# The last feed-forward stage: the high part of the weights passes once over 512 columns, and the bank's halves are added when it is read

## The chip, the cores and the metric

The kernel runs on one core of one Trainium2 chip. The metric is the device time of one execution in microseconds (us), the median of three runs. TensorE is called PE in the profile, VectorE DVE, ScalarE ACT, GpSimd POOL and SyncE SP.

## The reference

The reference is two model blocks in float32, one after the other, over 256 latent tokens of width 1024; the first also carries 256 context tokens. Each layer of the first block is a feed-forward, an attention and a feed-forward, each with a norm and with shifts, scales and gates made from a condition. Of its eleven parts only the feed-forward matters here:

```python
def rms(x):
    return x * lax.rsqrt(jnp.mean(x * x, axis=-1, keepdims=True) + EPS)

def modulate(h, shift, scale):
    return h * (1 + scale) + shift

def swiglu(h, wi, wo):                    # wi 1024 x 5632, wo 2816 x 1024
    g, u = jnp.split(h @ wi, 2, axis=-1)
    return (jax.nn.silu(g) * u) @ wo
```

The result is scaled by half of a gate and added to `x`. In the last layer of the first block the context isn't wanted any more after the attention, so the last feed-forward (`"post"`, layer 1) works on the 256 latent tokens alone. The second block (a recurrence, two sparse attentions and a table lookup of experts, twice) follows.

## The kernel before, in words

Tokens lie along the free dimension: `xT[:, m, :]` holds 128 features of 512 tokens, the latent ones first (`LAT` = 256), then the context (`TOK` = 512). The program is a chain of 27 stages. Each engine runs its own hand-written list, and all of them meet at the end of a stage (`end_phase`). The change touches one stage, number 9, `ffn("post", 1)`, the only feed-forward with `T == LAT`.

**Split products.** A float32 product is made of three matmuls in the type `fp32r`: operands are cut into a high part (`hi`, the rounded value) and a low part (`lo`, what is left), and w·h is w_hi·h_hi + w_hi·h_lo + w_lo·h_hi. `three` (L597) lists the pairs and `SplitWeights.mm` (L583, the matmul itself is L586) issues them into one PSUM bank. A block is one 128x128 piece of weights. A group is 8 blocks. ACT makes `w_hi` of a group (`SplitHi.ahead`, L539), DVE makes `w_lo` (`SplitLo.ahead`, L557), both four groups ahead of PE, in a ring of four (`split_ring`). A ring slot comes free when PE is two blocks into the next group. Weights come from HBM over SP's queue into `wt`, three tiles of two groups deep.

**The stage.** It has two halves of 33 groups. In a half, 11 pairs of groups come first: for each j, the gate (8 blocks over k, into a bank of `A_`) and the up projection (8 blocks, into a bank of `D_`). ACT applies silu to the gate's bank (L744), DVE multiplies it with the up bank (L761, `hid_raw`), ACT makes `hid_hi` (L750), DVE makes `hid_lo` (L768). Then 11 groups of the down projection: 8 outputs m, each 11 blocks over f, into banks of `D_`; the first m waits for each `hid_ready`. DVE adds each output to `xT` (`dve_residual`, L496). `h_hi` and `h_lo` have room for 512 columns; with `T == LAT` half of each is unused.

**Order on DVE and ACT.** Both lists go over the groups g in order. In an even g ACT takes silu of this gate and then splits group g+4; DVE only splits. In an odd g DVE multiplies, splits, and makes `hid_lo`; ACT splits and makes `hid_hi`. `step` (the `Stepper`) makes DVE or ACT wait for its own instruction to be done before it goes on, and other engines are told by `sem_inc` instructions behind it:

```python
step(dve.tensor_tensor(hid_raw[:, 0:T], s[:, 0:T], bank[:, 0:T], ALU.mult))
dve.sem_inc(silu_ring.free, 1)
dve.sem_inc(D_.free, 1)
dve.sem_inc(raw_ready.sem, 1)
```

Of the kernel before, what the change touches and what calls it, by code (L numbers as in the profile page):

```python
# [8 lines left out]
F32 = mybir.dt.float32  # L9
# [3 lines left out]
ALU = mybir.AluOpType  # L13
# [263 lines left out]
def model_kernel(nc, wstream, adastream, cond, vecs, consts, onehots, tokens, peer_uv, out):  # L277
    ctx = ExitStack()
    with ctx:
# [231 lines left out]
        w_hi_ready = signal("w_hi_ready")  # L511
        h_hi_ready = signal("h_hi_ready")
        raw_ready = signal("raw_ready")

        def groups_of(name, layer, cols, col=0):

# [45 lines left out]
        class SplitWeights:  # L562
# [20 lines left out]
            def mm(self, o, pairs, start, stop, inc):  # L583
# [5 lines left out]
                elif self.owed and not start:  # L589
                    ins.then_inc(split_ring.free, 1)  # L590
                    self.owed -= 1

            def close(self):
# [92 lines left out]
        def dve_split_norm(dve, step, groups, T):  # L686
            weights = SplitLo(dve, step, groups)
            dve.wait_ge(rstd_ready.sem, rstd_ready.due(dve))
            for k in range(DC + 2):
                if k < DC:  # L690
                    dve.tensor_tensor(hT[:, k, 0:T], xT[:, k, 0:T], rstd[:, 0:T], ALU.mult).then_inc(xn_ready.sem, 1)
                if k >= 2:
                    dve.wait_ge(h_hi_ready.sem, h_hi_ready.due(dve))
                    dve.tensor_tensor(h_lo[:, k - 2, 0:T], hT[:, k - 2, 0:T], h_hi[:, k - 2, 0:T].bitcast(F32),
                                      ALU.subtract).then_inc(h_ready.sem, 1)
# [11 lines left out]
        def pe_ffn(pe, W, mm, which, l, T):  # L707
            SW = SplitWeights(pe, W)
            pe_norm(pe, mm, T)
            for part in range(0, FC, HALF):  # L710
                for j in range(part, part + HALF):
                    for half, r in ((0, A_), (1, D_)):
                        pe.wait_ge(r.free, r.given_back())
                        bank = r.claim()
                        for k in range(DC):
                            if j == 0 and half == 0:
                                pe.wait_ge(h_ready.sem, h_ready.due(pe))
                            w = SW.next(f"ffn_{which}_wi", l, k * P, half * FF + j * P)
                            SW.mm(bank[:, 0:T], three(w, h_parts(k, 0, T)), k == 0, k == DC - 1,
                                  r.full if k == DC - 1 else None)  # L720
                for m in range(DC):
                    pe.wait_ge(D_.free, D_.given_back())
                    bank = D_.claim()
                    for f in range(HALF):
# [3 lines left out]
                        SW.mm(bank[:, 0:T], three(w, (hid_hi[:, f, 0:T], hid_lo[:, f, 0:T])), f == 0, f == HALF - 1,  # L728
                              D_.full if f == HALF - 1 else None)
            SW.close()  # L730

        def act_ffn(act, step, which, l, sub, T, first=False):
            if first:
                act.wait_ge(cond_loaded, 16)
                act.activation(silu_cc[:, :, :], silu_cc[:, :, :], ACT.Silu).then_inc(silu_done, 1)
                act.wait_ge(loaded.sem, loaded.due(act, FIRST_LOADS))
            weights = act_split_norm(act, step, ffn_groups(which, l), l, sub, T, first)
            for g in range(2 * HALF_GROUPS):
                i = g % HALF_GROUPS
                if i < GATED_GROUPS and i % 2 == 0:  # L740
                    act.wait_ge(A_.full, A_.filled())
                    act.wait_ge(silu_ring.free, silu_ring.given_back())
                    bank, s = A_.take(), silu_ring.claim()
                    step(act.activation(s[:, 0:T], bank[:, 0:T], ACT.Silu))  # L744
                    act.sem_inc(A_.free, 1)
                    act.sem_inc(silu_ring.full, 1)
                weights.ahead()
                if i < GATED_GROUPS and i % 2:
                    act.wait_ge(raw_ready.sem, raw_ready.due(act))
                    act.activation(hid_hi[:, i // 2, 0:T], hid_raw[:, 0:T], ACT.Copy).then_inc(hid_hi_ready.sem, 1)  # L750

        def dve_ffn(dve, step, which, l, sub, T, ada=(), first=False):
            ada = spread(ada, 2 * HALF_GROUPS)
            weights = (dve_first_norm if first else dve_split_norm)(dve, step, ffn_groups(which, l), T)
            for g in range(2 * HALF_GROUPS):
                i = g % HALF_GROUPS
                if i < GATED_GROUPS and i % 2:
                    dve.wait_ge(silu_ring.full, silu_ring.filled())
                    dve.wait_ge(D_.full, D_.filled())
                    s, bank = silu_ring.take(), D_.take()  # L760
                    step(dve.tensor_tensor(hid_raw[:, 0:T], s[:, 0:T], bank[:, 0:T], ALU.mult))  # L761
                    dve.sem_inc(silu_ring.free, 1)
                    dve.sem_inc(D_.free, 1)
                    dve.sem_inc(raw_ready.sem, 1)
                weights.ahead()
                if i < GATED_GROUPS and i % 2:
                    dve.wait_ge(hid_hi_ready.sem, hid_hi_ready.due(dve))
                    step(dve.tensor_tensor(hid_lo[:, i // 2, 0:T], hid_raw[:, 0:T],  # L768
                                           hid_hi[:, i // 2, 0:T].bitcast(F32), ALU.subtract))
                    dve.sem_inc(hid_ready.sem, 1)  # L770
                for m in range(DC):
                    if ((m + 1) * HALF - 1) // GROUP == i - GATED_GROUPS:
                        dve.wait_ge(D_.full, D_.filled())
                        dve_residual(dve, D_.take(), m, l, sub, T)
                dve_ada(dve, step, ada[g])


# [1840 lines left out]
```

## Time and profile before

| | us |
|---|---|
| median of three runs (lowest, highest) | 4734.04 (4729.76, 4736.26) |
| the profiled execution | 4733.32 |
| its span in the trace | 4731.5 |
| PE busy, 17932 matmuls | 4067.5 (86%) |
| DVE busy | 2743.8 (58%) |
| ACT busy | 1685.7 (36%) |
| stage 9: first split matmul to the last residual's end | 1889.5 to 2087.3 |

The span is cut by stages that have different limits, so the shares of the whole say little about one stage. The chain of waits is followed back from the last instruction; in stage 9 it is to be read in its own window. A matmul's listed duration is longer than its distance to the next one, because matmuls are pipelined: what a matmul costs in a stream is the distance from start to start. An instruction's idle time in brackets is how long its engine stood before it, with what ended that.

### The profile page before, as it was taken

The numbers are of one execution on the slowest core, as the hardware profiler recorded it, in microseconds if no ns is written. First come the engines' busy times: TensorE is split into PE (matmuls) and PEld (weight loads), VectorE is DVE, ScalarE is ACT, GpSimd is POOL, SyncE is SP. The second block draws the span as 40 slices with busy tenths as digits, with TensorE's granted clock in tenths as the row PEclk, the third lists the DMA queues.
The fourth block names the chain that finished last, engine by engine and source line by source line (L and its number), as shares of the span: only waits on it lengthen the run. The fifth ranks groups of instructions, "written<-read, shape, count | busy, mean of one in ns | idle before, by whom it ended". The sixth has DMA issues, their size and how long they took to land.

```text
span 4731.5 us, 53081 instructions
## 1 busy us (share of the span) xinstructions
PE 4067.5 (86%) x17932; PEld 2881.6 (61%) x17932; DVE 2743.8 (58%) x5474; ACT 1685.7 (36%) x3669; POOL 631.2 (13%) x665
## 2 busy tenths in 40 slices
PE   4998988999899887997888988877778889897777
PEld 3886755788688655996766844222367659542222
DVE  6776455666555456545335576777454355667774
ACT  3223434422322334432124444444321144344443
POOL 1000000000000000000000044444200000344442
PEclk7999987999999999998966999999989659999999
DMA  5444100444333202440121399999611214899997
GB/s 205 178 178 142 63 27 36 142 167 168 115 134 128 84 27 76 176 177 18 54 72 72 134 402 420 420 420 420 280 44 46 80 43 163 344 420 420 420 420 311
DMA packets 135023, 904.44 MB, mean 191 GB/s; under 512 B 14855, under 2 KB 15879, under 8 KB 35168
## 3 DMA queue, kind: packets, MB, share of 16 engines
q0 software_dynamic: 95552, 620.97, 32.4%
q1 hardware_dynamic: 39200, 280.08, 16.3%
q8 instruction: 143, 2.34, 0.2%
q14 instruction: 128, 1.05, 0.1%
HBM read 899.90 MB, written 5.28 MB: 191 GB/s over the span
## 4 chain that ended last, share of the span: by engine, by line
PE 60%; DMA 18%; DVE 12%; ACT 7%; issue 3%; DVEq 1%; POOL 0%; another core or an unknown queue 0%; ACTq 0%; POOLq 0%
PE ps L586 37%; PE ps L423 16%; DMA arena<-peer_uv,arena 13%; PE ps L2211 6%; DMA silu_cc<-peer_uv,arena 4%; ACT hT L488 1%; DVE arena L2360 1%; ACT arena L2270 1%; DVE arena L640 1%; ACT L2266 1%; ACT h_hi L683 1%; DMA arena<-adastream 1%; DVE arena L994 1%; DVE w_lo L557 1%; DVE arena L1969 0%
## 5 line engine op out<-in xcount | busy, mean ns | idle before, releaser
L2211 PE MATMUL ps<-arena 128*128 128x512 f32 x1640 | 813.2, 624 | 182.0 <-ACT arena L2270 181.0
L557 DVE TENSOR_TENSOR w_lo<-wt,w_hi 128x1024 fp32r<-128x1024 f32 x404 | 495.1, 1226 | 503.4 <-ACT w_hi L539 493.6
L586 PE MATMUL ps<-h_hi,w_hi 128*128 128x512 f32 (+1 forms) x1744 | 653.6, 375 | 93.2 <-DVE h_lo L663 50.3
L2333 POOL DMA_INDIRECT arena<-peer_uv,arena x410 | 442.6, 1080 | 1901.9 <-DVEq L2324 1310.7
L539 ACT ACTIVATE w_hi<-wt 128x1024 fp32r<-128x1024 f32 x404 | 422.5, 1058 | 762.9 <-PE ps L586 735.1
L2360 DVE CUSTOM_DVE_ANT_0 arena<-arena 128x1024 f32<-128x1024 f32 x410 | 502.5, 1226 | 320.4 <-DMA arena<-peer_uv,arena 318.9
L2211 PEld LDWEIGHTS ps<-arena 128*128 128x128 f32 x1640 | 295.0, 193 | 625.9 <-ACT arena L2270 395.5
L586 PE MATMUL ps<-h_lo,w_hi 128*128 128x512 f32 (+1 forms) x1744 | 642.1, 368 | 0.0
L586 PE MATMUL ps<-h_hi,w_lo 128*128 128x512 f32 (+1 forms) x1744 | 641.7, 368 | 0.0
L586 PEld LDWEIGHTS ps<-h_hi,w_hi 128*128 128x128 f32 x1744 | 334.1, 192 | 168.8 <-issue 89.5
L423 PE MATMUL ps<-arena 128*64 128x128 f32 (+5 forms) x1760 | 338.7, 368 | 55.9 <-ACTq L1953 21.5
L586 PEld LDWEIGHTS ps<-h_hi,w_lo 128*128 128x128 f32 x1744 | 334.9, 192 | 53.1
L586 PEld LDWEIGHTS ps<-h_lo,w_hi 128*128 128x128 f32 x1744 | 335.2, 192 | 51.5 <-issue 1.0
L423 PE MATMUL ps<-hT,wt 128*128 128x256 f32 x1376 | 342.0, 390 | 14.5 <-ACT hT L1251 10.0
L423 PEld LDWEIGHTS ps<-hT,wt 128*128 128x128 f32 x1376 | 264.7, 196 | 114.5 <-issue 74.5
L2266 ACT ACTIVATE arena<-arena 128x1 f32<-128x1 f32 x512 | 103.1, 201 | 628.4 <-DVE arena L2360 624.4
L423 PEld LDWEIGHTS ps<-arena 128*64 128x64 f32 (+3 forms) x1760 | 216.9, 190 | 131.0 <-issue 40.8
L625 POOL DMA_DIRECT2D ada_t<-adastream x133 | 70.6, 532 | 1498.1 <-DVEq L642 1086.7
L586 PE MATMUL ps<-hid_hi,w_hi 128*128 128x512 f32 (+1 forms) x704 | 255.4, 363 | 0.6 <-DVEq L770 0.6
L586 PE MATMUL ps<-hid_lo,w_hi 128*128 128x512 f32 (+1 forms) x704 | 255.2, 362 | 0.0
L586 PE MATMUL ps<-hid_hi,w_lo 128*128 128x512 f32 (+1 forms) x704 | 255.2, 362 | 0.0
L2270 ACT ACTIVATE arena<-cst,arena 128x128 f32<-128x128 f32 x512 | 205.5, 401 | 45.3 <-PE ps L2211 29.5
(319 smaller groups left out, 5926.1 us busy)
## 6 DMA issues: line engine op xcount, KB each, us to landing
wt<-wstream SPq DMA_DIRECT2D x262, 1024.0 KB
ada_t<-adastream POOLq DMA_DIRECT2D x133, 512.0 KB, 3.5
arena<-peer_uv,arena POOLq DMA_INDIRECT x410
arena<-adastream POOLq DMA_DIRECT2D x11, 512.0 KB, 26.5
bias_by_query<-bias_by_distance POOLq DMA_DIRECT2D x1, 4096.0 KB, 16.2
arena<-bias_by_query POOLq DMA_DIRECT2D x1, 3072.0 KB, 11.9
xT<-tokens SPq DMA_DIRECT2D x1, 2048.0 KB, 15.1
cst<-consts SPq DMA_DIRECT2D x1, 1816.0 KB, 8.9
```

Of the source, the lines that this page charges most:

```text
L423: ins = pe.matmul(o, lhsT, rhs, start=start, stop=stop, **kw)
L488: ins = act.activation(seg, seg, ACT.Identity, bias=mod[:, l, 3 * which * DC + k, r:r + 1], scale=mod[:, l, (3 * which + 1) * DC + k, r:r ...
L539: self.act.activation(hi, raw_group(g), ACT.Copy).then_inc(w_hi_ready.sem, 1)
L557: self.step(self.dve.tensor_tensor(lo, raw_group(g), hi.bitcast(F32), ALU.subtract))
L586: ins = self.pe.matmul(o, a, b, start=start and i == 0, stop=stop and i == 2)
L625: pool.dma_start(ada_t[:, i % 2, :], adastream[l * ADA_BLOCKS + m]).then_inc(ada_full[i % 2], 16)
L640: step(dve.tensor_tensor_reduce(product, w, silu_cc[:, r, :], 1.0, 0.0, ALU.mult, ALU.add, mod[:, l, m, r:r + 1]))
L2211: ins = pe.matmul(bank, diag[n % DIAGS], row[:, at:at + 512], start=s == 0, stop=s == SLOTS - 1)
L2266: step(act.activation(a[:, 0:1], hbuf[:, t, s:s + 1], ACT.Gelu))
L2270: act.activation(diag[n % DIAGS], ident, ACT.Copy, scale=a[:, 1:2]).then_inc(diag_ready.sem, 1)
L2333: pool.indirect_dma_start(out=rows[n % GB], out_offset=None, in_=peer_uv, in_offset=bass.IndirectOffsetOnAxis(ap=experts[:, t, s:s + 1], a ...
L2360: dve.tensor_tensor_reduce(u, u, ztok[:, t], 1.0, 0.0, ALU.mult, ALU.add, hbuf[:, t, s:s + 1]).then_inc(dot_ready.sem, 1)
```

## The change

In stage 9 alone (`T == LAT`):

- `h_lo` and `hid_lo` are written into columns 256 to 511 of `h_hi` and `hid_hi` (`lo_part`). A block is then two matmuls: w_hi over all 512 columns, and w_lo over the first 256 (`mm_wide`). The left half of a bank then holds w_hi·h_hi + w_lo·h_hi, the right half w_hi·h_lo.
- The halves are added when a bank is read. The gate: DVE sums with a `tensor_reduce` over pairs 256 columns apart into the silu buffer, and ACT applies silu there (it read PSUM before). The up projection: a `tensor_reduce` into `hid_raw`, then the product. The residual: two `scalar_tensor_tensor`, one per half.
- ACT splits the group before it waits for the gate's sum, and DVE sums the gate behind its split of the same g.

```diff
+        def dve_residual_wide(dve, step, bank, m, l, which):
+            seg, by = xT[:, m, 0:LAT], mod[:, l, (3 * which + 2) * DC + m, 0:1]
+            step(dve.scalar_tensor_tensor(out=seg, in0=bank[:, 0:LAT], scalar=by, in1=seg, op0=ALU.mult, op1=ALU.add))
+            dve.scalar_tensor_tensor(out=seg, in0=bank[:, LAT:TOK], scalar=by, in1=seg, op0=ALU.mult,
+                                     op1=ALU.add).then_inc(D_.free, 1)
...
+            def mm_wide(self, o, w, wide, start, stop, inc):
+                parts = [(o[:, 0:TOK], w[0], wide, start), (o[:, 0:LAT], w[1], wide[:, 0:LAT], False)]
+                for i, (to, a, b, first) in enumerate(parts[::-1] if stop else parts):
+                    ins = self.pe.matmul(to, a, b, start=first, stop=stop and i == 1)
...
+        def lo_part(hi, lo, k, T):
+            return hi[:, k, LAT:TOK] if T == LAT else lo[:, k, 0:T]
...
+        G_ = ring("gate_wide", [ps[:, 4 + i, :] for i in range(4)])
...
 def pe_ffn
-                            SW.mm(bank[:, 0:T], three(w, h_parts(k, 0, T)), k == 0, k == DC - 1,
-                                  r.full if k == DC - 1 else None)
+                            inc = r.full if k == DC - 1 else None
+                            if T == LAT:
+                                SW.mm_wide(bank, w, h_hi[:, k, :], k == 0, k == DC - 1, inc)
+                            else:
+                                SW.mm(bank[:, 0:T], three(w, h_parts(k, 0, T)), k == 0, k == DC - 1, inc)
...
 def act_ffn
+                    if T == LAT:
+                        weights.ahead()
+                        act.wait_ge(sum_ready.sem, sum_ready.due(act))
+                        s = silu_ring.claim()
+                        step(act.activation(s[:, 0:T], s[:, 0:T], ACT.Silu))
...
 def dve_ffn
+                    if T == LAT:
+                        step(dve.tensor_reduce(hid_raw[:, 0:T], bank.rearrange("p (r t) -> p t r", r=2), AX, ALU.add))
+                        step(dve.tensor_tensor(hid_raw[:, 0:T], s[:, 0:T], hid_raw[:, 0:T], ALU.mult))
...
                 weights.ahead()
+                if i < GATED_GROUPS and i % 2 == 0 and T == LAT:
+                    dve.wait_ge(G_.full, G_.filled())
+                    bank, s = G_.take(), silu_ring.bufs[silu_ring.taken % 3]
+                    step(dve.tensor_reduce(s[:, 0:T], bank.rearrange("p (r t) -> p t r", r=2), AX, ALU.add))
+                    dve.sem_inc(G_.free, 1)
+                    dve.sem_inc(sum_ready.sem, 1)
```

The order on DVE in the gated part of stage 9, one pair of groups of the kernel before (L557 splits weights, L761 is the product, L768 makes `hid_lo`):

```order
L557 TENSOR_TENSOR w_lo<-wt,w_hi 128x1024 [waits dve_chain,w_hi_ready]
L761 TENSOR_TENSOR hT<-hT,ps 128x256 [waits dve_chain,psd_full,silu_full]
L557 TENSOR_TENSOR w_lo<-wt,w_hi 128x1024 [waits dve_chain,w_hi_ready]
L768 TENSOR_TENSOR hid_lo<-hT,hid_hi 128x256 [waits dve_chain,hid_hi_ready]
```

The same pair in the changed kernel (L565 splits, L811 and L800 sum the gate's and the up projection's bank, L801 is the product, L816 makes the low part of `hid`):

```order
L565 TENSOR_TENSOR w_lo<-wt,w_hi 128x1024 [waits dve_chain,w_hi_ready]
L811 TENSOR_REDUCE hT<-ps 128x256 [waits dve_chain,gate_wide_full]
L800 TENSOR_REDUCE hT<-ps 128x256 [waits dve_chain,psd_full,silu_full]
L801 TENSOR_TENSOR hT<-hT 128x256 [waits dve_chain]
L565 TENSOR_TENSOR w_lo<-wt,w_hi 128x1024 [waits dve_chain,w_hi_ready]
L816 TENSOR_TENSOR hid_hi<-hT,hid_hi 128x256 [waits dve_chain,hid_hi_ready]
```

Two reductions are new, and the second waits for ACT's silu, which in turn waits for the first.

On ACT the same place before (L744 is silu, L539 splits, L750 makes `hid_hi`):

```order
L744 ACTIVATE hT<-ps 128x256 [waits silu_free,psa_full]
L539 ACTIVATE w_hi<-wt 128x1024 [waits act_chain,split_free,w_full2]
L539 ACTIVATE w_hi<-wt 128x1024 [waits split_free,w_full2]
L750 ACTIVATE hid_hi<-hT 128x256 [waits raw_ready]
```

and in the changed kernel (L547 splits, L776 is silu, L788 makes `hid_hi`):

```order
L547 ACTIVATE w_hi<-wt 128x1024 [waits split_free,w_full1]
L776 ACTIVATE hT<-hT 128x256 [waits sum_ready]
L547 ACTIVATE w_hi<-wt 128x1024 [waits act_chain,split_free,w_full1]
L788 ACTIVATE hid_hi<-hT 128x256 [waits raw_ready]
```

Silu has moved behind the first split, and waits for DVE instead of PE.

## Rows read from the trace of the kernel before

**Rows 1.** The page: the chain that ended last, by engine, share of span.

```profile
PE 60%; DMA 18%; DVE 12%; ACT 7%; issue 3%; DVEq 1%; POOL 0%; another core or an unknown queue 0%; ACTq 0%; POOLq 0%
```

**Rows 2.** Busy us and instructions of each engine in a stretch of stage 9.

```profile
core 0: us, PE busy (x) PEld busy (x) DVE busy (x) ACT busy (x) POOL busy (x), PEclk, DMA share, GB/s
1902.00:1952.00 50.00, 50.00 (x419) 50.00 (x418) 28.04 (x34) 25.06 (x36) 0.00 (x0) 1.00 0.48 170
```

**Rows 3.** Chain of waits through stage 9: start, us, what.

```profile
1889.51 70.23 PE ps L586 x534
...
1959.83 1.07 ACT w_hi L539
...
1960.92 1.24 DVE w_lo L557
...
1962.40 0.44 DVE hid_lo L768
...
1962.93 92.43 PE ps L586 x768
...
2058.46 28.34 PE ps L586 x234
...
2086.82 0.48 DVE xT L496
```

**Rows 4.** Groups by line and form, 1885 to 2100 us: busy, mean ns, idle.

```profile
L557 DVE TENSOR_TENSOR w_lo<-wt,w_hi 128x1024 fp32r<-128x1024 f32 x64 | 78.5, 1226 | 68.2 <-ACT w_hi L539 68.0
...
L768 DVE TENSOR_TENSOR hid_lo<-hT,hid_hi 128x256 fp32r<-128x256 f32 x22 | 9.4, 426 | 4.7 <-DVE w_lo L557 3.1
L761 DVE TENSOR_TENSOR hT<-hT,ps 128x256 f32<-128x256 f32 x22 | 9.3, 421 | 6.5 <-DVE w_lo L557 5.7 <-PE ps L586 0.8
L750 ACT ACTIVATE hid_hi<-hT 128x256 fp32r<-128x256 f32 x22 | 8.8, 399 | 0.0
...
L496 DVE SCALAR_TENSOR_TENSOR xT<-ps,mod,xT 128x256 f32<-128x256 f32 x16 | 7.7, 484 | 10.0 <-PE ps L586 7.2 <-DVE w_lo L557 1.6
```

**Rows 5.** DVE in order of time, gated part: start, us, what, idle before.

```profile
1930.69 0.42 DVE L761 TENSOR_TENSOR hT<-hT,ps 128x256 f32<-128x256 f32 x1 [0.22 <-DVE w_lo L557]
...
1936.45 0.42 DVE L761 TENSOR_TENSOR hT<-hT,ps 128x256 f32<-128x256 f32 x1 [0.22 <-DVE w_lo L557]
1937.88 1.23 DVE L557 TENSOR_TENSOR w_lo<-wt,w_hi 128x1024 fp32r<-128x1024 f32 x1 [1.01 <-ACT w_hi L539]
1939.36 0.42 DVE L768 TENSOR_TENSOR hid_lo<-hT,hid_hi 128x256 fp32r<-128x256 f32 x1 [0.25 <-DVE w_lo L557]
```

**Rows 6.** DVE in order of time, stage 1: a step without increments.

```profile
561.41 0.48 DVE L844 SCALAR_TENSOR_TENSOR arena<-hT,vec 128x256 f32<-128x256 f32 x1 [2.61 <-ACTq L829]
561.93 0.48 DVE L846 SCALAR_TENSOR_TENSOR hT<-hT,vec 128x256 f32<-128x256 f32 x1
```

**Rows 7.** All engines in order of time, stage 10: ACT hands over to DVE.

```profile
2093.47 0.42 ACT L459 ACTIVATE rstd<-rstd 128x256 f32<-128x256 f32 x1
2094.11 1.09 DVE L477 TENSOR_TENSOR hT<-xT,rstd 128x256 f32<-128x256 f32 x3 [6.81 <-ACTq L469]
```

**Rows 8.** Groups by form, whole run: reductions on DVE.

```profile
L2321 DVE TENSOR_REDUCE arena<-arena 128x32 f32<-128x512 f32 x32 | 21.8, 682 | 0.1
L994 DVE TENSOR_REDUCE arena<-ps 128x2 f32<-128x1024 f32 x16 | 19.6, 1225 | 14.5 <-PE ps L423 12.7 <-DVE hT L1017 1.7
L994 DVE TENSOR_REDUCE arena<-ps 128x2 f32<-128x512 f32 x16 | 11.1, 692 | 4.2 <-DVE hT L1017 3.7 <-DVE arena L1009 0.5
...
L1972 DVE TENSOR_REDUCE arena<-arena 128x2 f32<-128x256 f32 x16 | 6.7, 420 | 2.3
```

**Rows 9.** ACT in order of time, stage 5 (512 tokens): one pair apart.

```profile
1304.90 0.62 ACT L750 ACTIVATE hid_hi<-hT 128x512 fp32r<-128x512 f32 x1
...
1315.78 0.62 ACT L750 ACTIVATE hid_hi<-hT 128x512 fp32r<-128x512 f32 x1
```

**Rows 10.** PE in order of time around an idle stretch of 5.99 us.

```profile
1595.85 0.39 PE L586 MATMUL ps<-hid_hi,w_lo 128*128 128x512 f32 x1
1602.22 1.19 PE L423 MATMUL ps<-hT,cst 128*128 128x512 f32 x1 [5.99 <-ACT hT L671]
```

**Rows 11.** Stretches behind that idle time, columns as in Rows 2.

```profile
1602.20:1606.70 4.50, 4.47 (x6) 1.92 (x7) 0.00 (x0) 4.50 (x9) 0.00 (x0) 0.50 0.04 16
1606.70:1610.70 4.00, 4.00 (x11) 1.85 (x10) 3.54 (x3) 2.80 (x3) 0.00 (x0) 0.99 0.13 16
```

More of the change, by code:

```diff
@@ L513, in model_kernel @@
         raw_ready = signal("raw_ready")
+        sum_ready = signal("sum_ready")
         def groups_of(name, layer, cols, col=0):
@@ L591, in mm @@
                     self.owed -= 1
+            def mm_wide(self, o, w, wide, start, stop, inc):
+                parts = [(o[:, 0:TOK], w[0], wide, start), (o[:, 0:LAT], w[1], wide[:, 0:LAT], False)]
+                for i, (to, a, b, first) in enumerate(parts[::-1] if stop else parts):
+                    ins = self.pe.matmul(to, a, b, start=first, stop=stop and i == 1)
+                if inc is not None:
+                    ins.then_inc(inc, 1)
+                elif self.owed and not start:
+                    ins.then_inc(split_ring.free, 1)
+                    self.owed -= 1
             def close(self):
@@ L693, in dve_split_norm @@
                     dve.wait_ge(h_hi_ready.sem, h_hi_ready.due(dve))
-                    dve.tensor_tensor(h_lo[:, k - 2, 0:T], hT[:, k - 2, 0:T], h_hi[:, k - 2, 0:T].bitcast(F32),
+                    dve.tensor_tensor(lo_part(h_hi, h_lo, k - 2, T), hT[:, k - 2, 0:T], h_hi[:, k - 2, 0:T].bitcast(F32),
                                       ALU.subtract).then_inc(h_ready.sem, 1)
@@ L711, in pe_ffn @@
                 for j in range(part, part + HALF):
-                    for half, r in ((0, A_), (1, D_)):
+                    for half, r in ((0, G_ if T == LAT else A_), (1, D_)):
                         pe.wait_ge(r.free, r.given_back())
@@ L727, in pe_ffn @@
                         w = SW.next(f"ffn_{which}_wo", l, (part + f) * P, m * P)
-                        SW.mm(bank[:, 0:T], three(w, (hid_hi[:, f, 0:T], hid_lo[:, f, 0:T])), f == 0, f == HALF - 1,
-                              D_.full if f == HALF - 1 else None)
+                        inc = D_.full if f == HALF - 1 else None
+                        if T == LAT:
+                            SW.mm_wide(bank, w, hid_hi[:, f, :], f == 0, f == HALF - 1, inc)
+                        else:
+                            SW.mm(bank[:, 0:T], three(w, (hid_hi[:, f, 0:T], hid_lo[:, f, 0:T])), f == 0, f == HALF - 1,
+                                  inc)
             SW.close()
@@ L740, in act_ffn @@
                 if i < GATED_GROUPS and i % 2 == 0:
[L741 to L745, printed above, removed]
+                    if T == LAT:
[3 more added lines that the diff above has]
+                        step(act.activation(s[:, 0:T], s[:, 0:T], ACT.Silu))
+                    else:
+                        act.wait_ge(A_.full, A_.filled())
+                        act.wait_ge(silu_ring.free, silu_ring.given_back())
+                        bank, s = A_.take(), silu_ring.claim()
+                        step(act.activation(s[:, 0:T], bank[:, 0:T], ACT.Silu))
+                        act.sem_inc(A_.free, 1)
                     act.sem_inc(silu_ring.full, 1)
-                weights.ahead()
+                if T == TOK or i >= GATED_GROUPS or i % 2:
+                    weights.ahead()
                 if i < GATED_GROUPS and i % 2:
@@ L760, in dve_ffn @@
                     s, bank = silu_ring.take(), D_.take()
-                    step(dve.tensor_tensor(hid_raw[:, 0:T], s[:, 0:T], bank[:, 0:T], ALU.mult))
+                    if T == LAT:
+                        step(dve.tensor_reduce(hid_raw[:, 0:T], bank.rearrange("p (r t) -> p t r", r=2), AX, ALU.add))
+                        step(dve.tensor_tensor(hid_raw[:, 0:T], s[:, 0:T], hid_raw[:, 0:T], ALU.mult))
+                    else:
+                        step(dve.tensor_tensor(hid_raw[:, 0:T], s[:, 0:T], bank[:, 0:T], ALU.mult))
                     dve.sem_inc(silu_ring.free, 1)
@@ L765, in dve_ffn @@
                 weights.ahead()
+                if i < GATED_GROUPS and i % 2 == 0 and T == LAT:
[4 more added lines that the diff above has]
+                    dve.sem_inc(sum_ready.sem, 1)
                 if i < GATED_GROUPS and i % 2:
                     dve.wait_ge(hid_hi_ready.sem, hid_hi_ready.due(dve))
-                    step(dve.tensor_tensor(hid_lo[:, i // 2, 0:T], hid_raw[:, 0:T],
+                    step(dve.tensor_tensor(lo_part(hid_hi, hid_lo, i // 2, T), hid_raw[:, 0:T],
                                            hid_hi[:, i // 2, 0:T].bitcast(F32), ALU.subtract))
@@ L773, in dve_ffn @@
                         dve.wait_ge(D_.full, D_.filled())
-                        dve_residual(dve, D_.take(), m, l, sub, T)
+                        if T == LAT:
+                            dve_residual_wide(dve, step, D_.take(), m, l, sub)
+                        else:
+                            dve_residual(dve, D_.take(), m, l, sub, T)
                 dve_ada(dve, step, ada[g])
```

## The prediction

> **What bounds the kernel now.** I read the page's chain first: PE carries 60% of it [rows 1], so PE's instruction stream is the thing to follow. Then the stretch table of stage 9: in 50 us PE issues 419 matmuls and is busy throughout, at the full clock of 2.4 GHz, while DVE is busy 28 us and ACT 25 [rows 2]. The chain through the stage says the same: it runs on PE's matmuls from 1889.51 to 2086.82 us, and leaves them only twice, where the down projection waits for the last low part of `hid` (PE's matmuls go on at 1962.93 and at 2058.46) [rows 3]. At each of these the path goes over ACT's split, DVE's split and DVE's `hid_lo`, and the matmuls around it lie about 0.5 us further apart than their count asks for. So PE is the bound, and DVE comes close once per half. The reader should see in the groups that DVE's idle time lies before L557 and is ended by ACT [rows 4]: ACT may only split when PE has given a slot back, so DVE is paced by PE and has time to spare, how much the cycle below tells.
>
> DVE's order of time gives that cycle: the product L761 comes at 1930.69 and again at 1936.45, 5.76 us for a pair of groups, which is 48 matmuls of 256 columns, **0.120 us each** [rows 5]. In stage 5, with 512 columns, a pair takes from 1304.90 to 1315.78, 10.88 us, **0.227 us each** [rows 9].
>
> **What the change takes from PE.** Stage 9 has 66 groups of 8 blocks, 528 blocks. Each loses two matmuls of 256 columns and gains one of 512: 2 x 0.120 - 0.227 = 0.013 us. The columns that pass are the same 768; what goes is the fixed part of one matmul. Over 528 blocks that is 7.0 us. A block takes 0.347 us instead of 0.360, a pair 5.55 instead of 5.76. The Trainium skill ("TensorE: Matmul & The Clock Gate", Back-to-back issue gap) gives the distance as columns over 2.4 GHz plus 2.5 ns; by that the saving would be an estimated 2.5 ns a block and 1.3 us in all. The rows show 13 ns beyond the columns at both widths, so I keep 7.0.
>
> **What it puts on DVE.** Per pair of groups DVE's list now is split, sum of the gate, sum of the up bank, product, split, low part, each with a wait for itself, and between the two sums ACT's silu. Durations: two splits at 1.226, the product 0.42, the low part 0.43 [rows 4]. A reduction of 512 elements from PSUM takes 0.692 with 2 results, and one in SBUF 0.682 with 32 results; 256 elements take 0.420 and 1024 take 1.225 [rows 8]. The time goes with the elements read and not with the results, so I take 0.69 for each sum, with 0.42 and 1.225 as ends, since none of these rows has 256 results or reads its pairs 256 columns apart. Silu from SBUF I cost like L750, 0.40 [rows 4]. That is 2.45 + 1.38 + 0.42 + 0.43 + 0.40 = 5.08 us.
>
> Between them stand the waits. A step with nothing behind it costs 0.04 (561.89 to 561.93) [rows 6]; with the semaphore increments of a split behind it 0.22 and 0.25 [rows 5]; ACT to DVE with two increments 0.22 (2093.89 to 2094.11) [rows 7]. So about 0.1 for each increment instruction. Split to gate sum 0.22, gate sum to silu (two increments) 0.22, silu to up sum (one) 0.15, up sum to product (none) 0.04, product to split (three) 0.33, split to low part 0.25, low part to split (one) 0.20: 1.41 us. The cycle is **5.08 + 1.41 = 6.49 us**. PE needs 5.55. DVE's list, with silu inside it, is then slower than PE, and becomes the bound of the gated part. The ring of four groups hides nothing of it, since the down projection needs the last low part: what DVE is late by at the end of 11 pairs, PE stands still for.
>
> **The sum.** First half: DVE's first split begins where it does now, in step with the first group, and 11 cycles follow. Today 11 x 5.76 = 63.4 us bring PE back at 1962.93 [rows 3]; with 6.49 they take 71.4, +8.0. Second half, from there to PE's return at 2058.46, today 95.5 us [rows 3]. New: PE has 78 blocks of the down projection left (88 less the first ten), 27.0; one group of gate, 2.8; from its end to DVE's first split 2.0 (two blocks until the slot comes free, 0.7, and some 0.2 until ACT sees it, then ACT's copy to DVE's start, 1959.83 to 1960.92, 1.1 [rows 3]); 11 cycles less the last gap, 71.2; and 0.1 to PE. That is 103.1, +7.6. End: 78 blocks save 1.0, and the last residual's second half adds 0.48 + 0.04 [rows 4, 6]: -0.5. The other residuals cost nothing: in the down projection DVE has 1.23 + 0.2 + 2 x 0.48 + 0.15 = 2.5 us of work in a group of 2.77, and that cover is thin but whole. ACT's split stands first now and is not late: silu needs DVE's sum, which comes behind DVE's split of what ACT has just copied. No DMA is moved, and the weights' queue gets more time. Together +8.0 + 7.6 - 0.5 = **+15.1 us**.
>
> **The clock.** At the turn to the down projection PE has done f = 9 and waits one whole cycle less a block for f = 10, 6.49 - 0.35 = 6.1 us idle, in both halves. The trace has such a case: PE idle for 5.99 us before 1602.22 [rows 10], then 4.5 us at a granted clock of 0.50 (1.2 GHz) before it is back at 0.99 [rows 11]. Half of 4.5 us is lost, 2.25 each, 4.5 for both. By itself this has the ends 0 (the clock doesn't fall) and 6.
>
> Forecast: +15.1 + 4.5 = +19.6 us on the profiled execution's 4733.3, which stands 0.7 below the median of the three runs. That gives 4752.9; I say **4753**.
>
> **Rivals.**
> - *PE stays the bound, and it gets faster.* If the gaps between DVE's instructions were nothing, the cycle would be 5.08, under PE's 5.55; the gain is 7.0 less 0.5 for the last residual, 4733.3 - 6.5 = 4726.8. The point of decision: below 5.55 all of it comes, and at 5.80 it is used up (27.0 + 2.8 + 2.0 + 11 x 5.80 - 0.1 = 95.5). Against it stand 0.22 and 0.25 in every pair [rows 5]; they are instructions between the steps, and the new list has more of them. The Trainium skill ("VectorE: DVE Perf Modes", Rules for kernel authors) advises to lower the number of operations of a chain and not that of semaphores, by which the increments would be free. The rows speak against that. Chance 0.08.
> - *Cheap sums.* If a sum costs like 256 elements, 0.42, the cycle is 5.95: 22 x 0.54 = 11.9 less, +3.2 and the clock's 4.5, 4741. Within the bound of no change. Every reduction in the trace is paid by what it reads. Chance 0.10.
> - *Dear sums.* 256 results of two elements each, 1 KB apart, are in no row. At 0.90 each the cycle is 6.91: 22 x 0.42 = +9.2, 4762; at 1.225 it is 22 x 1.07 = +23.5, 4776. Chance 0.15.
> - *The clock stays up.* Then 4748.4; it belongs to the forecast's own range.
> - *The change doesn't do what it says.* Its order has 528 matmuls of 512 and 528 of 256 columns in the stage, so it does; no chance is kept for it.
>
> **How the numbers follow.** Forecast 0.67, which with gaps off by 0.15 a cycle (3.3 us) and the clock at 0 to 6 reaches from 4745 to 4758. With part of the cheap and of the dear case the range is 4740 to 4770. A measurement of this kernel tells 0.2%, 9.5 us, from no change. Faster by more than that would need more than PE has to give (7.0), so even the first rival hardly gets there: 0.03. Within it (4724.5 to 4743.5) lie that rival and most of the cheap sums: 0.17. Slower 0.80.
>
> **What would show it.** In the profile after: 528 matmuls fewer; PE in the gated part no longer busy throughout, with waits on DVE's w_lo (about 0.9 us a pair); L811 a cycle of 6.49 us apart; L811 and L800 at 0.69; two PE idles of some 6 us before the down projection, and a granted clock of 0.50 behind them; the down projection at 0.347 us a block; stage 9 some 20 us longer and every other stage as it was. The prediction is wrong if PE is busy throughout the gated part, if the sums take other than 0.65 to 0.75, or if the cycle lies under 5.8.

## The result and the profile after

The changed kernel takes 4758.22 us (median of five executions, lowest 4754.43) against 4734.04, a ratio of 1.0050 (95% interval 1.0034 to 1.0066): slower by 24 us. One of the five executions, 5315 us at a mean granted clock of 0.72, was disturbed and is no part of the ratio; the median of the other four is 4757.4, slower by 23.4. Measured again later (last experiment) it took 4754.21, a ratio of 1.0039 (1.0025 to 1.0053), slower by 18. The profiled execution took 4754.43, 21.1 us more than the one of before.

The page of the changed kernel, span and busy time by engine:

```profile
span 4752.6 us, 52085 instructions
...
PE 4070.2 (86%) x17404; PEld 2856.4 (60%) x17404; DVE 2781.7 (59%) x5534; ACT 1686.5 (35%) x3669; POOL 622.6 (13%) x665
```

There are 528 matmuls fewer (17932 to 17404), and PE isn't busy any less; DVE has 38 us more to do. How long stage 9 is can be read from ACT, whose first instruction in it and in stage 10 is a table load (L454). In order of time on ACT, before:

```profile
1876.86 1.28 ACT L454 ACT_TABLE_LOAD   x1 [10.23 <-DVEq L381]
...
2087.38 1.28 ACT L454 ACT_TABLE_LOAD   x1 [10.59 <-DVEq L381]
```

and after:

```profile
1877.10 1.28 ACT L454 ACT_TABLE_LOAD   x1 [10.23 <-DVEq L381]
...
2103.77 1.28 ACT L454 ACT_TABLE_LOAD   x1 [10.89 <-DVEq L381]
```

The stage grew from 210.5 to 226.7 us, by 16.2. All the experiments below are read by this length first. In the same kernel it hardly moves (226.7 in both profiles of the changed kernel), while whole executions of one kernel lie up to 10.5 us apart.

DVE in the gated part after, in order of time, one pair of groups; it answers to [rows 5]:

```profile
1931.73 1.23 DVE L565 TENSOR_TENSOR w_lo<-wt,w_hi 128x1024 fp32r<-128x1024 f32 x1
1933.11 0.69 DVE L811 TENSOR_REDUCE hT<-ps 128x256 f32<-128x512 f32 x1
1934.47 0.69 DVE L800 TENSOR_REDUCE hT<-ps 128x256 f32<-128x512 f32 x1 [0.68 <-ACTq L783]
1935.20 0.43 DVE L801 TENSOR_TENSOR hT<-hT 128x256 f32<-128x256 f32 x1
1935.97 1.22 DVE L565 TENSOR_TENSOR w_lo<-wt,w_hi 128x1024 fp32r<-128x1024 f32 x1 [0.34 <-ACT w_hi L547]
1937.43 0.43 DVE L816 TENSOR_TENSOR hid_hi<-hT,hid_hi 128x256 fp32r<-128x256 f32 x1 [0.24 <-DVE w_lo L565]
1938.00 1.23 DVE L565 TENSOR_TENSOR w_lo<-wt,w_hi 128x1024 fp32r<-128x1024 f32 x1
```

The cycle is 1938.00 - 1931.73 = 6.27 us. No gap in it is ended by PE: what ends the gaps is DVE itself or ACT, which in turn waits for DVE. Before, the split in this place waited 1.01 us for ACT, and ACT for PE [rows 5].

The groups of the stage after, by line and form, answer to [rows 4]:

```profile
L565 DVE TENSOR_TENSOR w_lo<-wt,w_hi 128x1024 fp32r<-128x1024 f32 x64 | 78.4, 1225 | 34.0 <-ACT w_hi L547 29.9 <-DVE hT L801 0.7
...
L800 DVE TENSOR_REDUCE hT<-ps 128x256 f32<-128x512 f32 x22 | 15.2, 692 | 14.9 <-ACTq L783 14.9
L811 DVE TENSOR_REDUCE hT<-ps 128x256 f32<-128x512 f32 x22 | 15.2, 691 | 4.2 <-DVE w_lo L565 2.4 <-PE ps L605 0.2
...
L776 ACT ACTIVATE hT<-hT 128x256 f32<-128x256 f32 x22 | 9.2, 418 | 62.3 <-DVEq L813 62.3
```

A sum takes 0.69 us. The time for which the split waits has halved (68.2 to 34.0 us), and some 19 us of what is left lie in the down projection. And ACT's silu waits 62.3 us for DVE: that is ACT's spare time, not a loss.

PE in the down projection's first output (the second row is f = 10), in order of time with its idle time in brackets:

```profile
1962.46 0.47 PE L605 MATMUL ps<-hid_hi,w_hi 128*128 128x512 f32 x1 [0.39 <-DVEq L566]
1969.30 0.58 PE L605 MATMUL ps<-hid_hi,w_lo 128*128 128x256 f32 x1 [5.65 <-DVEq L818]
```

and stretches around it (us, busy time and count of PE, PEld, DVE, ACT, POOL, then the granted clock):

```profile
1963.30:1969.30 6.00, 0.35 (x3) 0.04 (x2) 4.45 (x6) 2.84 (x4) 0.00 (x0) 0.68 0.48 175
1969.30:1972.20 2.90, 2.90 (x9) 2.52 (x10) 1.23 (x1) 0.00 (x0) 0.00 (x0) 0.50 0.80 280
1972.20:1976.20 4.00, 4.00 (x25) 3.48 (x23) 1.43 (x2) 1.06 (x1) 0.00 (x0) 1.00 0.16 64
```

PE stands for 5.65 us until DVE's increment behind the last `hid_lo`, and then passes nine matmuls in 2.9 us at half clock where it passes 25 in 4.0 at the full clock. In the second half it stands 5.65 us too, and goes on at 0.50 from 2072.3 to 2078.0.

Up to there PE hardly waits. The stretch table of the gated part, and from the list of waits in the stage the stands at f = 10 (us in total, times, longest):

```profile
1902.00:1952.00 50.00, 49.61 (x282) 42.89 (x282) 36.98 (x49) 22.96 (x32) 0.00 (x0) 1.00 0.43 153
```

```profile
PE ps L605 <- DVEq L818: 11.3, 2, 5.7
```

PE waits for a split group for the first time at 1949.93, and then once in a cycle until the gated part ends: three times 0.39 us in the first half, four times 0.44 to 0.49 in the second, 3.0 us in all against the 11.3 at f = 10. Until then the groups split ahead cover what DVE is late by, and most of the loss is paid in one stand at the end. So PE's busy time in a stretch of the gated part doesn't tell which engine is the bound; DVE's cycle and the stand at f = 10 do.

### The profile page after: what moved, and what is told of

The parts are those of the page before. It is cut to its first block, busy times and chain, and to the rows that moved or that the text cites. A ratio compares the mean times of both kernels' runs of the same rounds, so it can differ in the third digit from the quotient of the medians.

```text
span 4752.6 us, 52085 instructions
## 1 busy us (share of the span) xinstructions
PE 4070.2 (86%) x17404; PEld 2856.4 (60%) x17404; DVE 2781.7 (59%) x5534; ACT 1686.5 (35%) x3669; POOL 622.6 (13%) x665
## 4 chain that ended last, share of the span: by engine, by line
PE 57%; DMA 17%; DVE 14%; ACT 6%; issue 4%; DVEq 1%; another core or an unknown queue 0%; ACTq 0%; POOL 0%; POOLq 0%
PE ps L594 33%; PE ps L423 16%; DMA arena<-peer_uv,arena 12%; PE ps L2262 6%; DMA silu_cc<-peer_uv,arena 4%; PE ps L605 2%; DVE w_lo L565 2%; ACT hT L488 1%; DVE arena L2411 1%; DVE arena L663 1%; ACT arena L2321 1%; ACT h_hi L706 1%; DVE arena L1045 1%; DVE arena L2020 0%; DMA arena<-adastream 0%
## 5 line engine op out<-in xcount | busy, mean ns | idle before, releaser
L565 DVE TENSOR_TENSOR w_lo<-wt,w_hi 128x1024 fp32r<-128x1024 f32 x404 | 495.0, 1225 | 468.2 <-ACT w_hi L547 454.5
L547 ACT ACTIVATE w_hi<-wt 128x1024 fp32r<-128x1024 f32 x404 | 422.2, 1057 | 724.4 <-PE ps L594 651.5
L594 PE MATMUL ps<-h_hi,w_hi 128*128 128x512 f32 (+1 forms) x1392 | 550.2, 395 | 90.0 <-DVE h_lo L686 51.2
L594 PE MATMUL ps<-h_lo,w_hi 128*128 128x512 f32 (+1 forms) x1392 | 540.2, 388 | 0.0
L594 PE MATMUL ps<-h_hi,w_lo 128*128 128x512 f32 (+1 forms) x1392 | 539.8, 388 | 0.0
L594 PEld LDWEIGHTS ps<-h_hi,w_hi 128*128 128x128 f32 x1392 | 264.9, 190 | 163.0 <-issue 84.3
L594 PEld LDWEIGHTS ps<-h_hi,w_lo 128*128 128x128 f32 x1392 | 265.1, 190 | 52.9
L594 PEld LDWEIGHTS ps<-h_lo,w_hi 128*128 128x128 f32 x1392 | 265.4, 191 | 51.5 <-issue 1.0
L594 PE MATMUL ps<-hid_hi,w_hi 128*128 128x512 f32 x528 | 205.4, 389 | 0.0
L594 PE MATMUL ps<-hid_lo,w_hi 128*128 128x512 f32 x528 | 205.4, 389 | 0.0
L594 PE MATMUL ps<-hid_hi,w_lo 128*128 128x512 f32 x528 | 205.4, 389 | 0.0
## 6 DMA issues: line engine op xcount, KB each, us to landing
xT<-tokens SPq DMA_DIRECT2D x1, 2048.0 KB, 15.1
```

What stands on the lines that cost most here:

```text
L547: self.act.activation(hi, raw_group(g), ACT.Copy).then_inc(w_hi_ready.sem, 1)
L565: self.step(self.dve.tensor_tensor(lo, raw_group(g), hi.bitcast(F32), ALU.subtract))
L594: ins = self.pe.matmul(o, a, b, start=start and i == 0, stop=stop and i == 2)
```

## The experiments

The theory that they test: in the gated part the changed kernel is bound by DVE's list, which is one chain with silu in it; PE's saving is real and hidden behind it; and the fall of the clock has a price of its own. "Stage" is the length of stage 9 by ACT's table loads, less the 210.5 us of before; "whole" is the median less that of the kernel before measured along with it; the last column is the ratio of the executions with its 95% interval.

| experiment | stage | median us | whole | ratio |
|---|---|---|---|---|
| the change (the four undisturbed) | +16.2 | 4757.4 | +23.4 | 1.0050 (1.0034 to 1.0066) |
| PE's part alone | -3.8 | 4732.8 | -1.4 | 0.9999 (0.9990 to 1.0008) |
| DVE's part alone | +17.0 | 4757.9 | +23.8 | 1.0049 (1.0035 to 1.0063) |
| silu waited for later | +10.2 | 4748.3 | +14.2 | 1.0030 (1.0018 to 1.0042) |
| right halves by ACT | -3.4 | 4732.8 | -1.3 | 0.9997 (0.9988 to 1.0006) |
| PE alone, widths in pairs | -5.7 | 4730.8 | -4.6 | 0.9992 (0.9983 to 1.0001) |
| right halves by ACT, last pair first | -4.4 | 4731.9 | -3.4 | 0.9994 (0.9985 to 1.0003) |
| the change, PE kept busy | +12.2 | 4751.1 | +15.7 | 1.0032 (1.0020 to 1.0044) |
| by ACT, last pair first, in pairs | -6.4 | 4728.9 | -6.4 | 0.9987 (0.9978 to 0.9996) |
| kernel before, stage 9 delayed by 11 | +10.9 | 4746.5 | +10.7 | 1.0022 (1.0013 to 1.0031) |
| delayed by 15 | +15.0 | 4753.6 | +17.8 | 1.0039 (1.0025 to 1.0053) |
| delayed by 19 | +19.1 | 4755.7 | +19.9 | 1.0042 (1.0028 to 1.0055) |
| the change again | +16.2 | 4754.2 | +18.4 | 1.0039 (1.0025 to 1.0053) |

**PE's part alone.** Silu, product and residual read the left half of the bank only, in the order of before.

```diff
-                        step(dve.tensor_reduce(hid_raw[:, 0:T], bank.rearrange("p (r t) -> p t r", r=2), AX, ALU.add))
-                        step(dve.tensor_tensor(hid_raw[:, 0:T], s[:, 0:T], hid_raw[:, 0:T], ALU.mult))
...
+                    step(dve.tensor_tensor(hid_raw[:, 0:T], s[:, 0:T], bank[:, 0:T], ALU.mult))
...
+                        act.wait_ge(G_.full, G_.filled())
+                        act.wait_ge(silu_ring.free, silu_ring.given_back())
+                        bank, s = G_.take(), silu_ring.claim()
+                        step(act.activation(s[:, 0:T], bank[:, 0:T], ACT.Silu))
```

> PE's part of the change alone: a block is the 512-wide and the 256-wide matmul, but only the left half of each bank is read, with the order and the single reads of the kernel before. Left out of the computation: the product of the weights' high part with the tokens' low part, so the output lacks it. Theory (DVE's list made the change slow, PE's saving is real): 528 blocks x 0.013 us = 7.0 us under the kernel before, 4727, PE busy throughout the gated part, a pair at 5.55 us, the clock up. Rival (the wide pass itself is dear, or reading a bank of which both halves are being made): at or above the kernel before, 4734 to 4755.

The stage is 3.8 us shorter, not 7.0. The stretch table of this kernel, gated part:

```profile
1905.00:1955.00 50.00, 50.00 (x285) 43.49 (x284) 29.01 (x35) 25.28 (x36) 0.00 (x0) 1.00 0.50 175
```

PE is busy throughout, and passes 284 matmuls (one was under way) in 50 us: 0.176 each, 0.352 a block of two. DVE's products, which PE paces here, lie 5.64 us apart (1910.34 to 1955.46 for eight pairs), 0.3525 us a block. The saving over 0.360 is 0.0075 us a block, 4.0 us over 528 blocks. So PE's saving is real, and in sign the theory holds, but the term was too large: I had added the distances of two pure streams, 0.120 and 0.227 [rows 5, 9], and the mixed stream costs 6 ns a block more. In the whole the 3.8 us are not to be told from nothing (-1.4, ratio 0.9999), so that PE's saving is shown by the stage and not by the time of the kernel.

**DVE's part alone.** The halves are summed as in the change, but filled with three matmuls of 256 columns:

```diff
+                if start:
+                    parts = [(o[:, 0:TOK], w[0], wide, True), (o[:, 0:LAT], w[1], wide[:, 0:LAT], False)]
+                else:
+                    parts = [(o[:, 0:LAT], w[0], wide[:, 0:LAT], False), (o[:, LAT:TOK], w[0], wide[:, LAT:TOK], False),
+                             (o[:, 0:LAT], w[1], wide[:, 0:LAT], False)]
```

> DVE's part of the change alone: the halves are summed as in the changed kernel, but PE fills them with three matmuls of 256 columns (the first block of a bank stays wide, since it opens the bank). Theory: DVE's cycle of 6.27 us hides PE's loss in the gated part (5.74 us a pair), which only shows in the down projection, 2 x 78 blocks x 0.013 less the openers = +2 us over the changed kernel, 4760. Rival (the wide pass is the cost): back towards the kernel before, 4734 to 4740. Third reading (PE's saving counts in full everywhere): +6 us, 4764.

4757.9 us, the same as the change; the stage is 0.9 us longer than there. With the saving measured above, 2 x 78 blocks of the down projection less the 14 that open a bank make 142 x 0.0075 = 1.1 us. The saving shows only where DVE isn't the bound. The rival that blamed the wide pass is out: with or without it the change costs the same.

**Silu waited for later.** One wait is moved on DVE; the operations stay.

```diff
-                    dve.wait_ge(silu_ring.full, silu_ring.filled())
...
                     dve.wait_ge(D_.full, D_.filled())
...
                         step(dve.tensor_reduce(hid_raw[:, 0:T], bank.rearrange("p (r t) -> p t r", r=2), AX, ALU.add))
+                        dve.wait_ge(silu_ring.full, silu_ring.filled())
                         step(dve.tensor_tensor(hid_raw[:, 0:T], s[:, 0:T], hid_raw[:, 0:T], ALU.mult))
```

> The changed kernel with DVE's wait for silu moved behind the sum of the up bank; same operations. Theory (the list in series is the bound): the path gate sum, silu, up sum (0.18 + 0.42 + 0.07 us) is replaced by a gap with two increments, about 0.24, so the cycle falls from 6.27 to 5.84 us; 22 x 0.43 = 9.5 us less, and the idle before the down projection falls from about 6 to 4.5 us, so up to 4 us more if the clock stays up: 4745 to 4749. Rival (DVE's busy time and not the order is what counts, or the time is lost on PE): less than 2 us, 4756 to 4758.

6.0 us less in the stage and about 9 in the whole, with the same operations on DVE: the order is what counts. DVE in order of time in this kernel:

```profile
1934.23 0.69 DVE L815 TENSOR_REDUCE hT<-ps 128x256 f32<-128x512 f32 x1
1935.16 0.69 DVE L801 TENSOR_REDUCE hT<-ps 128x256 f32<-128x512 f32 x1 [0.24 <-DVE hT L815]
1935.88 0.42 DVE L805 TENSOR_TENSOR hT<-hT 128x256 f32<-128x256 f32 x1
1936.79 1.23 DVE L565 TENSOR_TENSOR w_lo<-wt,w_hi 128x1024 fp32r<-128x1024 f32 x1 [0.48 <-ACT w_hi L547]
...
1940.20 0.69 DVE L815 TENSOR_REDUCE hT<-ps 128x256 f32<-128x512 f32 x1
```

The gap before the second sum is 0.24 in place of 0.68, as expected, and the cycle is 5.97, not 5.84: before the split there are now 0.48 us in place of 0.34, ended by ACT. ACT copies that group only after silu, and silu starts when the gate's sum is there; with DVE faster, this second way round the loop ends last. PE's idle at f = 10 fell to 4.69 and 5.09 us, and the clock still fell behind it (granted 0.50 from 1970.0 to 1974.6): the part of the expectation that had it stay up was wrong. The stage gave 6.0 us where 9.5 and more was expected; that the median still lies in the expected range comes from outside the stage. PE is busy throughout the gated part of this kernel, though DVE is its bound, as the two stands at f = 10 show:

```profile
2000.00:2050.00 50.00, 50.00 (x286) 43.45 (x285) 38.35 (x51) 22.84 (x33) 0.00 (x0) 1.00 0.50 178
```

```profile
PE ps L605 <- DVEq L822: 9.8, 2, 5.1
```

**Right halves by ACT.** ACT copies the right half of each gated bank to SBUF, DVE adds with a `tensor_tensor` over 256 elements, sums the gate before its split, and waits for silu behind the up sum.

```diff
+                        act.wait_ge(G_.full, gates)
+                        act.activation(part_g, G_.bufs[(gates - 1) % 4][:, LAT:TOK], ACT.Copy).then_inc(part_ready.sem, 1)
...
+                    dve.wait_ge(part_ready.sem, part_ready.due(dve))
...
+                    step(dve.tensor_tensor(s[:, 0:T], part_g, bank[:, 0:LAT], ALU.add))
...
+                        step(dve.tensor_tensor(hid_raw[:, 0:T], part_u, bank[:, 0:LAT], ALU.add))
```

> The wide pass kept; ACT, which has time to spare, copies the right half of each gated bank to SBUF, and DVE adds it to the left half with a tensor_tensor over 256 elements (0.42) in place of the reduction over 512 (0.69); DVE sums the gate before its split, so that silu lies beside the split, and waits for silu behind the up sum. Theory: the cycle would be 2 x 0.42 + 0.42 + 0.43 + 2 x 1.23 + gaps 1.2 = 5.3 us, under PE's 5.55: PE is the bound again, 7.0 us less than before and 0.5 more for the last residual: 4727 to 4729. Rival (ACT becomes the bound, or PE's saving isn't there): 4734 or more.

The stage is 3.4 us shorter than before, 19.6 shorter than with the change; PE is the bound again: DVE's products lie 5.64 us apart, as with PE's part alone, and the stands at f = 10 have shrunk from 11.3 us to 0.6:

```profile
PE ps L607 <- DVEq L837: 0.6, 2, 0.4
```

Nothing of the computation is left out here. The copies, the cheaper sums and the new order came in together; what each of them is worth isn't shown, beyond the 6.0 us of the moved wait. Only PE's own saving was smaller than the 7.0 on which the expectation stood.

**Widths in pairs.** PE's part alone, with every second block narrow first: wide, narrow, narrow, wide.

```diff
-                for i, (to, a, b, first) in enumerate(parts[::-1] if stop else parts):
+                for i, (to, a, b, first) in enumerate(parts[::-1] if stop or odd else parts):
```

> PE's part alone as in the run before of that kind (only the left half of each bank is read; the product of the weights' high part with the tokens' low part is left out), but every second block passes narrow first, so that PE's stream is wide, narrow, narrow, wide. There a block took 0.3525 us where the sum of the two pure streams is 0.347. Theory (what the mixed stream costs over the pure ones comes at a change of width): half as many changes, a block at 0.350, 1.5 us less over the stage. Rival (the wide pass is dearer here for another reason, as the place of its operands): 0.3525 as before, no change in the stage.

The stretch table of this kernel:

```profile
1905.00:1955.00 50.00, 50.00 (x289) 43.65 (x288) 29.24 (x35) 25.34 (x36) 0.00 (x0) 1.00 0.51 177
```

288 matmuls in 50 us are 0.347 a block, but a count of 288 is exact only to one. DVE's products lie 5.57 us apart (1910.52 to 1955.10 for eight pairs), 0.348 a block, and the stage is 1.8 us shorter than with PE's part alone. What the mixed stream cost hangs on the order of the widths. Over 0.3467, the sum of the pure streams, 5.8 ns a block have become 1.6 in the gated part, while the changes of width in a group of 8 blocks went from 14 to 8. A price per change would leave more; but in the whole stage only 1.8 of the 3.1 us went. What sets the cost isn't shown.

**Last pair first.** On the version with ACT's copies, `hid_hi` and `hid_lo` of the last pair come before the splits.

```diff
+                last = T == LAT and i == GATED_GROUPS - 1
+                if not last:
+                    weights.ahead()
...
+                if last:
+                    weights.ahead()
```

> The version with ACT's copies of the right halves; in the last pair of each half of the stage ACT makes hid_hi and DVE hid_lo before they split the next group. Theory: the last low part is ready before PE comes to f = 10, so the stand of 0.5 to 0.6 us in each half goes: 1.1 us less in the stage, 4731 to 4732, which the whole time hardly tells. Rival (something else holds PE there): no change in the stage.

0.9 us less in the stage, where 1.1 was expected, and no stand of PE at f = 10 is left; the whole can't tell it.

**PE kept busy.** The change, with 20 matmuls into an unread bank in each idle before f = 10.

```diff
+                        if T == LAT and m == 0 and f == HALF - 1:
+                            pe.wait_ge(G_.free, G_.given_back())
+                            for _ in range(20):
+                                pe.matmul(G_.bufs[G_.claimed % 4], w[0], hid_hi[:, 0, :], start=True, stop=True)
```

> The changed kernel, with 20 more matmuls of 512 columns into a bank that nobody reads, in each half of the stage while PE waits for f = 10 of the down projection (20 x 0.23 = 4.6 us of the 5.7 us idle). Nothing is left out. Theory (the fall of the clock behind this idle time costs its own share): the granted clock stays at 1.00, and 1.45 + 2.85 = 4.3 us come back: stage 4 us shorter, 4754. Rival (the clock is no part of the loss, or the filler delays the blocks behind it): 4758 or more.

PE around the same place in this kernel, and the stretches there:

```profile
1970.07 0.39 PE L605 MATMUL ps<-hid_hi,w_lo 128*128 128x256 f32 x1 [1.09 <-DVEq L822]
```

```profile
1970.00:1975.00 5.00, 4.93 (x28) 4.32 (x29) 2.27 (x2) 1.06 (x1) 0.00 (x0) 1.00 0.60 213
...
2071.00:2076.00 5.00, 4.31 (x24) 3.79 (x25) 2.04 (x4) 1.16 (x2) 0.00 (x0) 1.00 0.33 102
```

The granted clock stays at 1.00 and the stage is 4.0 us shorter than the change's, with the same wait for `hid_lo`. So the fall of the clock costs 4.0 of the 16.2 us.

**All of it together.** ACT's copies, last pair first, widths in pairs.

> Both last edits on the version with ACT's copies. Theory: 1.1 us from the last pair and 1.5 us from the order of widths, if that holds: stage 6 us shorter than before the change, 4728 to 4730. Rival: as the version with ACT's copies, 4733.

4728.93 us, 6.4 less than before, ratio 0.9987 (0.9978 to 0.9996): faster than both kernels, by little. Its stretch table:

```profile
1905.00:1955.00 50.00, 50.00 (x289) 43.65 (x288) 36.29 (x54) 32.30 (x56) 0.00 (x0) 1.00 0.48 172
```

PE waits for DVE nowhere in this stage, not at f = 10 either, though DVE is busy 36.3 us of 50, against 37.0 in the change: it was not DVE's busy time that made the change slow.

**Delays of the kernel before.** With a stage 9 longer by 16 the change's whole was longer by 23. To see whether starting the later stages later costs something itself, stage 9 of the kernel before was lengthened with matmuls on PE, 50, 67 and 84 in each half.

```diff
+                            pe.wait_ge(A_.free, A_.given_back())
+                            for _ in range(67):
+                                pe.matmul(A_.bufs[A_.claimed % 4][:, 0:LAT], w[0], hid_hi[:, 0, 0:LAT], start=True, stop=True)
```

> The kernel before, with 50 further matmuls of 256 columns in each half of stage 9, ahead of f = 10 of the down projection, into a bank that nobody reads; nothing is left out. It makes the stage 2 x 50 x 0.120 less the two stands of 0.5 = 11 us longer and leaves PE busy, the clock up, and DVE's and ACT's lists as before. What is asked: the kernels with a longer stage 9 lost more in the whole than in the stage (changed kernel: stage +16, whole +24). Theory (a later start of the later stages costs them something itself): whole +14 to +15, 4749. Rival (it came from the edits): whole +11, 4746.

> The same with 67 matmuls in each half: stage +15. Theory of the later start: whole +20 to +23, 4756. Rival: +15, 4750.

> The same with 84 matmuls in each half: stage +19. Theory of the later start: whole +22 to +28, 4760. Rival: +19, 4754.

The whole followed the stage: 10.7 for 10.9, 17.8 for 15.0, 19.9 for 19.1. The middle one is 2.8 over; there is no common surcharge for a late start.

> The changed kernel once more, as it is. Delaying stage 9 of the kernel before by 11, 15 and 19 us cost 11, 18 and 20 in the whole, so a later start is not what makes the changed kernel lose 24 us in the whole where its stage loses 16. If the excess is the scatter of a few executions, the median comes out lower this time, 4751 to 4755; if it belongs to the change, again at 4757 to 4759.

18.4 in the whole for 16.2 in the stage, so part of the first excess was scatter between executions. A part comes again. From the table load of stage 10 to the end of the span the profile of before takes 2644.1 us (4731.5 - 2087.38), and the two of the change take 2648.8 and 2648.9, 4.7 and 4.8 more. This stretch is longer by 3.5 to 7.2 us in the three other kernels in which DVE is the bound of stage 9 (7.2 with DVE's part alone, 3.5 with silu waited for later, 5.2 with PE kept busy), and by -0.8 to 2.5 in the eight that are left, the three delays among them. So the excess goes with the DVE-bound kernels, which are also those that sum with `tensor_reduce`, and not with a late start; what causes it isn't shown. Of the 4.7 us, 1.5 lie in the norm of stage 10, which in its first 3.9 us of matmuls had a granted clock of 0.56 where it was 1.00 before. That part is not the change's own: five other profiles have the same 1.5 us or more (widths in pairs, last pair first, PE kept busy, the delays by 15 and 19).

## Why the prediction was right, point by point

Forecast 4753, range 4740 to 4770, slower with 0.80; measured 4758.2 and 4754.2. Right in sign and in the mechanism of the sum: DVE's chain is longer than PE's cycle, the loss comes out at f = 10, and the clock falls behind it. That the size fits so well is partly luck: the stage was forecast 3.4 us too long, and the stages behind it, forecast as they were, took 4.7 us longer.

- **The bound.** PE before, DVE's list after: shown by DVE's order of time, and by the two halves of the change run apart (PE alone -3.8, DVE alone +17.0 in the stage).
- **The cycle**, forecast 6.49, is 6.27. The durations held (sums 0.69, splits 1.23, product and low part 0.43, silu 0.42 for 0.40). Mis-sized were the gaps, 1.41 forecast: split to sum 0.14 (0.22), sum to silu and silu to sum 0.26 together (0.37), low part to split 0.14 (0.20); product to split 0.34 and split to low part 0.24 held. With the 0.04 before the product they add up to 1.16. I took the gap behind a split, 0.22, from a place where the product has one wait more than the low part has [rows 5], and costed the others by it; in the kernel before the product comes 0.22 us behind a split with one increment and the low part 0.15, and 0.32 and 0.25 behind a split with two. Over 22 cycles the 0.22 us are 4.8 us too much.
- **PE's saving**, forecast 7.0 us, is 3.8 to 4.0: the term "0.120 and 0.227 added". In this change most of it was hidden, so its error entered with 78 blocks of each half only, 0.9 us.
- **The sum for the stage without the clock** was +15.1. From PE's returns: the first half took 6.1 us more (8.0 forecast). The second took 103.0 for 95.5, +7.5 with 1.45 of clock in it, so 6.1 (7.6 forecast); the end +2.5 with 2.85 of clock, so -0.3 (-0.5 forecast). Together 11.9.
- **The clock**, forecast 4.5 us, costs 4.0 by the kernel that keeps PE busy, and half of 2.9 + 5.7 us, 4.3, by the granted clock. The idle was 5.65 us each time where 6.1 was forecast.
- **The stage** is then +16.2 against +19.6; the rest of the 21.1 us between the two profiled executions came from outside of it, 4.7 of it from behind the stage. The prediction put that at nothing ("every other stage as it was"), and it came in both profiles of the change.
- **The signs.** Not all of them came. PE was to wait 0.9 us a pair in the gated part, and the prediction called itself wrong if PE is busy throughout it. PE was busy 49.61 of 50 us there and stood seven times for 0.39 to 0.49 us. That the ring hides nothing of the loss was right in the sum and wrong in the place: it moves the waiting to the end. The sign was badly chosen, since a DVE-bound kernel can meet it in full (silu waited for later, 50.00 of 50). The down projection runs at 0.352 us a block and not at 0.347. The others held: 528 matmuls fewer, sums of 0.69, two stands of nearly 6 us, and 0.50 behind them.
- **The rivals.** That PE stays the bound failed at the gaps: without them the cycle would have been 5.1 us. The Trainium skill ("VectorE: DVE Perf Modes", Rules for kernel authors) advises to lower a chain's operations and not its semaphores. In this trace the increments aren't free: a step costs 0.04 us to the next instruction with no increment behind it, 0.14 with one, 0.24 with two and 0.34 with three. Cheap and dear sums are out: 0.69, the time for the elements read. By the formula in the Trainium skill ("TensorE: Matmul & The Clock Gate", Back-to-back issue gap), columns over 2.4 GHz plus 2.5 ns, which the page gives for an isolated matmul, PE's saving would be an estimated 1.3 us; measured 3.8.

## What to carry to other kernels

An engine that is busy for three quarters of a stretch (DVE 37.0 of 50 us in the change) can still be its bound, if its list is a chain with another engine inside: add durations and gaps once round the loop and compare with the bound engine's cycle before giving the list more to do. If it comes out too long, first look at what an instruction waits for earlier than it must: moving one wait gave 6.0 us back, and together with ACT's copies and the gate's sum ahead of the split the whole loss, with the same work on PE. A ring that runs ahead hides such a bound from PE's busy time until its lead is used up, so look at the end of the part, where the engines must meet. And where one engine hands over to PE at the end of a part, an idle of some 5 us was paid again in clock here.

## What the runs showed of the hardware that I had not expected

- Matmuls of 512 and 256 columns in turn take 0.3525 us for the two, in the order wide, narrow, narrow, wide 0.348; the pure streams add up to 0.3467 (0.2267 and 0.120).
- A `tensor_reduce` that sums pairs 1 KB apart in PSUM to 256 results takes 0.69 us, like one with 2 results of 256 elements each [rows 8]: neither the number of results nor the stride cost anything here.
- Behind an idle of 4.7 to 5.7 us on PE the granted clock was 0.50 for 2.9 to 5.9 us after the return (the change, and silu waited for later); 20 matmuls into an unread bank kept it at 1.00 and brought 4.0 us back.
- An increment instruction costs DVE's list 0.10 us. In the second half of the stage it is the other split of a pair that has two increments, and the gate's sum stands 0.24 us behind it where it stood 0.15 in the first (1931.73 + 1.23 to 1933.11), while the low part goes from 0.24 to 0.14:

```profile
2055.03 0.69 DVE L811 TENSOR_REDUCE hT<-ps 128x256 f32<-128x512 f32 x1 [0.24 <-DVE w_lo L565]
```
